# Two-layer decoder trunk on one core: FFN gate and up products with the weights stationary in nine of eleven steps

## The chip, the cores and the metric

One core of one Trainium2 chip runs the whole kernel. The metric is device time in microseconds (us) of one execution. Engines are called as the profile calls them: PE is TensorE's matrix products, PEld its weight loads, DVE is VectorE, ACT is ScalarE, POOL is GpSimd and SP is SyncE, which issues the weight DMAs.

## The reference, cut to what matters

The input is 256 tokens of 1024 channels; there are two layers. A layer is: a SwiGLU FFN, a mixer with two kinds of attention, a second SwiGLU FFN, and a gated embedding. The change touches only the two FFNs of each layer:

```python
def swiglu(x, w_gu, w_down):
    g, u = jnp.split(x @ w_gu, 2, axis=-1)
    return (jax.nn.silu(g) * u) @ w_down

f = swiglu(rms_norm(h, ffn1_pre_g[i]), ffn1_w_gu[i], ffn1_w_down[i])
h = h + 0.5 * rms_norm(f, ffn1_post_g[i])
```

`w_gu` is 1024 x 5632 and `w_down` 2816 x 1024, all in float32. The row scale of `rms_norm`, one number r per token, is not applied to x: the kernel multiplies the results g and u by it. The channel gain is folded into the weights.

## The kernel before, in words

**Numbers.** A float32 matrix is split in two parts that the PE takes at its fast float32 form: `w_hi` is the rounded weight, `w_lo` the rest, and the same for x (`x_hi`, `x_lo`) and the gated product (`ht_hi`, `ht_lo`). `exact` (line 1336) makes three matmuls of each block: hi by hi (line 1338), hi by lo (line 1339), lo by hi (line 1340), accumulated in PSUM. Of a matmul's operands one is stationary, a 128 x 128 block that a weight load (PEld) puts into the array, and one is moving and streams through it column by column. Here x is stationary and the weights move, 512 columns a matmul, so every matmul has a load of its own.

**Tiling.** Tokens are 2 tiles of 128 (t). Weights come from HBM in units of 1 MB, in 3 slots of `raw`; SP loads unit u when the splitting of unit u - 3 is done. For each unit ACT makes `w_hi` (`high`, line 591) and DVE then `w_lo` (`low`, line 1002); ACT waits for `units_used`, that is for PE to be done with the unit that was in the slot. PE waits for `split_done` (`begin`, line 1367).

**The FFN's steps.** The 2816 hidden channels are 11 steps (NC) of 256. A step c is `step` (line 1457): `gate_up` on its first unit (k blocks 0 to 3 of 8), the transposes of step c - 1 (`turn_ht`), `gate_up` on its second unit (k blocks 4 to 7), and `down` of step c - 1. `gate_up` does 24 matmuls a unit: for t, for k, three. PSUM bank 4 gets tile 0 (256 columns of gate, 256 of up) and bank 5 gets tile 1. `down` is 24 more. Steps 2 to 9 are a hardware loop; the first and the last step are written out.

**The gated product.** When tile t is done, ACT computes silu(r g) from PSUM with r as its per-partition scale (`silu`, line 684), and DVE multiplies it by r u (`product`, line 1041): tokens are the partitions. `down` wants the hidden channels as partitions, so PE transposes the 128 x 256 product of both tiles with four 128 x 128 transposes (`turn_ht`, line 1409), ACT copies them rounded into `ht_hi` (`high_ht`, line 673) and DVE the rest into `ht_lo` (`low_ht`, line 1030).

**Order.** The order is written out by hand. In the loop ACT does: high of the down unit, `high_ht`, high of the next first unit, two `silu`, high of the next second unit. DVE does the same with `low`, `low_ht`, `product`.

Of the kernel before, what the change touches and what calls it, by code (L numbers as in the profile page):

```python
# [73 lines left out]
def trunk_kernel(nc, a, out):  # L74
    with ExitStack() as ctx:
# [3 lines left out]
        def sem(name):  # L79
            return ctx.enter_context(nc.semaphore(name))  # L80
# [496 lines left out]
        def _(act):  # L577
# [92 lines left out]
                high_inputs(i, q, 1, (1,))  # L670
                square_pre(i, n + 1, 1)

            def high_ht(i, f, c):
                act.wait_ge(ht_turned, 2 * HTS * i + HTS * f + c + 1)
                act.activation(ht_hi[:, :, :], bank(HT_BANK).rearrange("p (k n) -> p k n", k=2),  # L675
                               ACT.Copy).then_inc(ht_high, 1)

            def high_last_ht(i, f, t):
                toks = slice(t * P, (t + 1) * P)
                act.wait_ge(ht_turned, 2 * HTS * i + HTS * f + NC + t)  # L680
                act.activation(x_hi[:, 0:2, toks], bank(HT_BANK).rearrange("p (k n) -> p k n", k=2)[:, :, toks],
                               ACT.Copy).then_inc(ht_high, 1)

            def silu(i, f, step, u, t, c=0):
                wait_product(act, gu_done, 2 * NC * i + NC * f + step + 1, i, u, t, c)
                act.activation(glu[:, t, 0, :], bank(GU_BANK[t])[:, 0:FC], ACT.Silu,  # L686
                               scale=r_pre[:, t:t + 1]).then_inc(silu_done, 1)

            def ffn(i, f, u0, g0, next_unit, loads, embedding):

                act.wait_ge(pre_scale, 8 * i + 4 * f + 1)
                silu(i, f, 0, u0 + 1, 0)
# [5 lines left out]
                with act.Fori(1, NC - 1) as c:  # L698
# [3 lines left out]
                    for t in range(TT):  # L702
                        silu(i, f, c, u0, t, c)
# [5 lines left out]
                for t in range(TT):  # L709
                    silu(i, f, NC - 1, u0 + 3 * NC - 3, t)  # L710
                high_last_ht(i, f, 0)
                next_unit()
                high_last_ht(i, f, 1)
# [238 lines left out]
        def _(dve):  # L952
# [94 lines left out]
            def ffn(i, f, u0, g0, next_unit):  # L1047
                product(i, f, 0, 0)
                low(i, u0 + 3, g0 + 4, halves=(0,))
                product(i, f, 0, 1)  # L1050
                low(i, u0 + 3, g0 + 4, halves=(1,))
                with dve.Fori(1, NC - 1) as c:
                    low(i, u0 + 1, c=c)
                    low_ht(i, f, c - 1)
                    low(i, u0 + 2, g0, c=c)
                    for t in range(TT):
                        product(i, f, c, t)
# [4 lines left out]
                low_ht(i, f, NC - 2)  # L1062
# [270 lines left out]

        @block.tensor
        def _(pe):
            def exact(dst, x_h, x_l, w_h, w_l, first, last):

                pe.matmul(dst, x_h, w_h, start=first, stop=False)  # L1338
                pe.matmul(dst, x_h, w_l, start=False, stop=False)  # L1339
                return pe.matmul(dst, x_l, w_h, start=False, stop=last)  # L1340

            def wide(s, dst, xh, xl, k0, t, first, last, before=None):

# [62 lines left out]
                        elif s == 1 and done is not None:  # L1406
                            mm.then_inc(done, 1)

            def turn_ht(i, f, c):
                pe.wait_ge(prod_done, 4 * NC * i + 2 * NC * f + 2 * c + 2)  # L1410
                for k in range(2):
                    for t in range(TT):
                        mm = pe.transpose(bank(HT_BANK)[:, k * SEQ + t * P:k * SEQ + (t + 1) * P],  # L1413
                                          glu[:, t, 1, k * P:(k + 1) * P], ident[:, :])
                mm.then_inc(ht_turned, 1)
# [19 lines left out]
                return wait  # L1435

            def ffn(i, f, q, u0, before_last):
                def gate_up(u, half, step, c=0):

                    begin(i, u, c)  # L1440
                    for t in range(TT):
                        if half == 0:

                            pe.wait_ge(prod_done, 4 * NC * i + 2 * NC * f + 2 * step + t - 1)
                        mm = wide(slot(u), bank(GU_BANK[t]), x_hi, x_lo, 4 * half, t, half == 0, half == 1)
                        if half == 1 and t == 0:
                            mm.then_inc(gu_done, 1)
                    mm.then_inc(units_used, 1)
# [47 lines left out]
                turn_ht(i, f, NC - 2)  # L1496
# [277 lines left out]
```

## Time and profile before

| | us |
|---|---|
| median of 3 runs | 1201.45 (1201.3 to 1202.21) |
| the profiled execution, its own time | 1202.05 |
| its span, first to last instruction | 1200.3 |
| PE busy | 1185.5 |
| PEld busy | 968.0 |
| DVE busy | 753.5 |
| ACT busy | 684.5 |

The profiled execution took 1.75 us more than its span; this lies around the first and the last instruction. A matmul's duration in the profile runs from when it starts to when its last result is out, so durations of matmuls that follow each other overlap: the pace is read from starts, or from a stretch divided by the matmuls in it. PEld runs beside PE. In a timeline a row with xN merges N instructions of one line.

### The profile page before, as it was taken

The numbers are of one execution on the slowest core, as the hardware profiler recorded it, in microseconds if no ns is written. First come the engines' busy times: TensorE is split into PE (matmuls) and PEld (weight loads), VectorE is DVE, ScalarE is ACT, GpSimd is POOL, SyncE is SP. The second block draws the span as 40 slices with busy tenths as digits, with TensorE's granted clock in tenths as the row PEclk, the third lists the DMA queues.
The fourth block names the chain that finished last, engine by engine and source line by source line (L and its number), as shares of the span: only waits on it lengthen the run. The fifth ranks groups of instructions, "written<-read, shape, count | busy, mean of one in ns | idle before, by whom it ended". The sixth has DMA issues, their size and how long they took to land.

```text
span 1200.3 us, 15956 instructions
## 1 busy us (share of the span) xinstructions
PE 1185.5 (99%) x5585; PEld 968.0 (81%) x5585; DVE 753.5 (63%) x1086; ACT 684.5 (57%) x1122; POOL 91.5 (8%) x153
## 2 busy tenths in 40 slices
PE   8999999999999999999999999999999999999997
PEld 6888888877778888888878888878877888888886
DVE  5655656677667755565775555575966676555566
ACT  6644556666665654454674554475656756455455
POOL 3000000042000000000100000010600000000001
PEclk9999999999999999999999999999999999999999
DMA  7756555553345565655546555746344456555550
GB/s 259 231 186 203 178 194 198 194 175 118 129 176 175 179 193 188 200 180 206 176 146 207 181 194 182 240 163 202 121 138 141 175 175 211 176 179 193 185 193 35
DMA packets 138607, 215.33 MB, mean 179 GB/s; under 512 B 6914, under 2 KB 97860, under 8 KB 138564
## 3 DMA queue, kind: packets, MB, share of 16 engines
q1 hardware_dynamic: 135840, 208.70, 52.2%
q10 hardware_dynamic: 2660, 6.06, 1.5%
q8 instruction: 27, 0.44, 0.1%
q14 instruction: 16, 0.13, 0.0%
q0 software_dynamic: 64, 0.00, 0.0%
HBM read 213.68 MB, written 1.05 MB: 179 GB/s over the span
## 4 chain that ended last, share of the span: by engine, by line
PE 92%; DVE 3%; ACT 3%; issue 1%; DMA 1%; POOL 0%; SPq 0%; DVEq 0%; POOLq 0%; ACTq 0%
PE ps L1338 29%; PE ps L1340 28%; PE ps L1339 28%; DVE w_lo L1016 2%; PE ps L1413 1%; PE ps L1385 1%; ACT w_hi L607 1%; PE ps L1507 1%; ACT prob L740 1%; PE ps L1553 1%; DMA raw<-in_w_ple_proj 1%; PE ps L1540 0%; PE ps L1526 0%; ACT w_hi L604 0%; DVE neg_max L1195 0%
## 5 line engine op out<-in xcount | busy, mean ns | idle before, releaser
L1338 PE MATMUL ps<-w_hi,x_hi 128*128 128x512 f32 x1216 | 486.7, 400 | 1.4 <-DVE x_lo L1027 0.7
L1340 PE MATMUL ps<-w_hi,x_lo 128*128 128x512 f32 x1216 | 475.5, 391 | 0.0
L1339 PE MATMUL ps<-w_lo,x_hi 128*128 128x512 f32 x1216 | 474.2, 390 | 0.0
L1016 DVE SCALAR_TENSOR_TENSOR w_lo<-raw,g_layer,w_hi 128x512 fp32r<-128x512 f32 (+1 forms) x524 | 392.9, 808 | 82.9 <-ACT w_hi L607 82.1
L607 ACT ACTIVATE w_hi<-raw,g_layer 128x512 fp32r<-128x512 f32 (+1 forms) x524 | 346.5, 732 | 15.6 <-PE ps L1340 15.5
L1338 PEld LDWEIGHTS ps<-w_hi,x_hi 128*128 128x128 f32 x1216 | 228.5, 188 | 55.4 <-issue 5.3
L1340 PEld LDWEIGHTS ps<-w_hi,x_lo 128*128 128x128 f32 x1216 | 228.2, 188 | 49.2
L1339 PEld LDWEIGHTS ps<-w_lo,x_hi 128*128 128x128 f32 x1216 | 228.8, 188 | 43.7
L1013 DVE TENSOR_TENSOR w_lo<-raw,w_hi 128x1024 fp32r<-128x1024 f32 x114 | 134.6, 1221 | 81.6 <-ACT w_hi L604 81.6
L604 ACT ACTIVATE w_hi<-raw 128x1024 fp32r<-128x1024 f32 x114 | 114.7, 1052 | 103.5 <-PE ps L1340 103.5
L1338 PE MATMUL ps<-w_hi,ht_hi 128*128 128x512 f32 x320 | 125.0, 390 | 0.0
L1340 PE MATMUL ps<-w_hi,ht_lo 128*128 128x512 f32 x320 | 124.6, 389 | 0.0
L1339 PE MATMUL ps<-w_lo,ht_hi 128*128 128x512 f32 x320 | 124.5, 389 | 0.0
L675 ACT ACTIVATE ht_hi<-ps 128x512 fp32r<-128x512 f32 x40 | 23.9, 598 | 145.2 <-PE ps L1413 145.2
L1032 DVE TENSOR_TENSOR ht_lo<-ps,ht_hi 128x512 fp32r<-128x512 f32 x40 | 27.6, 691 | 112.3 <-ACT ht_hi L675 112.3
L686 ACT ACTIVATE glu<-ps,r_pre 128x256 f32<-128x256 f32 x88 | 41.1, 467 | 85.8 <-PE ps L1340 85.8
L1043 DVE SCALAR_TENSOR_TENSOR glu<-ps,r_pre,glu 128x256 f32<-128x256 f32 x88 | 42.3, 480 | 46.2 <-ACT glu L686 46.2
L1340 PEld LDWEIGHTS ps<-w_hi,ht_lo 128*128 128x128 f32 x320 | 60.1, 188 | 12.5
L1339 PEld LDWEIGHTS ps<-w_lo,ht_hi 128*128 128x128 f32 x320 | 60.1, 188 | 12.4
L1338 PEld LDWEIGHTS ps<-w_hi,ht_hi 128*128 128x128 f32 x320 | 60.1, 188 | 12.3
L639 ACT ACTIVATE x_hi<-ps 128x512 fp32r<-128x512 f32 x40 | 23.7, 595 | 37.6 <-PE ps L1385 37.6
L495 POOL TENSOR_TENSOR ms_post<-mean_post,eps_half 128x1 f32<-128x1 f32 x8 | 2.2, 271 | 555.8 <-ACT tmp L656 555.8
(193 smaller groups left out, 749.4 us busy)
## 6 DMA issues: line engine op xcount, KB each, us to landing
raw<-in_ffn_w_gu SPq DMA_DIRECT2D x170, 512.0 KB, 4.6
raw<-in_ffn_w_down SPq DMA_DIRECT2D x88, 512.0 KB, 4.0
raw<-in_w_in SPq DMA_DIRECT2D x80, 512.0 KB, 4.5
raw<-in_w_out SPq DMA_DIRECT2D x16, 512.0 KB, 3.7
raw<-in_w_ple_gate SPq DMA_DIRECT2D x16, 512.0 KB, 4.1
raw<-in_w_branch_sb SPq DMA_DIRECT2D x8, 512.0 KB, 3.7
raw<-in_w_branch_diff SPq DMA_DIRECT2D x8, 512.0 KB, 3.8
raw<-in_ffn_w_gu SPq DMA_DIRECT2D x12, 256.0 KB, 7.2
```

Of the source, the lines that this page charges most:

```text
L604: last = act.activation(w_hi[:, s, part], raw[:, s, part], ACT.Copy)
L607: last = act.activation(w_hi[:, s, part], raw[:, s, part], ACT.Copy, scale=g_layer[:, g:g + 1])
L639: act.activation(x_hi[:, 4 * n:4 * n + 4, t * P:(t + 1) * P], x_bank(i, q, idx).rearrange("p (k n) -> p k n", k=4), ACT.Copy).then_inc(x_h ...
L675: act.activation(ht_hi[:, :, :], bank(HT_BANK).rearrange("p (k n) -> p k n", k=2), ACT.Copy).then_inc(ht_high, 1)
L686: act.activation(glu[:, t, 0, :], bank(GU_BANK[t])[:, 0:FC], ACT.Silu, scale=r_pre[:, t:t + 1]).then_inc(silu_done, 1)
L1013: last = dve.tensor_tensor(w_lo[:, s, part], raw[:, s, part], whi[:, part], ALU.subtract)
L1016: last = dve.scalar_tensor_tensor(out=w_lo[:, s, part], in0=raw[:, s, part], scalar=g_layer[:, g:g + 1], in1=whi[:, part], op0=ALU.mult, o ...
L1032: dve.tensor_tensor(ht_lo[:, :, :], bank(HT_BANK).rearrange("p (k n) -> p k n", k=2), ht_hi[:, :, :].bitcast(F32), ALU.subtract).then_inc( ...
L1043: dve.scalar_tensor_tensor(out=glu[:, t, 1, :], in0=bank(GU_BANK[t])[:, FC:2 * FC], scalar=r_pre[:, t:t + 1], in1=glu[:, t, 0, :], op0=ALU ...
L1338: pe.matmul(dst, x_h, w_h, start=first, stop=False)
L1339: pe.matmul(dst, x_h, w_l, start=False, stop=False)
L1340: return pe.matmul(dst, x_l, w_h, start=False, stop=last)
```

## The change

In steps 1 to 9 of each FFN (36 of the 44 steps of the whole kernel) gate and up are computed the other way round: the weights are the stationary operand, 128 hidden channels at a time, and x moves, all 256 tokens. `flat_gate_up` goes over four groups j of 128 hidden channels in a unit (two of gate, into bank 4, two of up, into bank 5) and the four k blocks, with three 256-column matmuls each: 48 matmuls a unit and not 24. The result has the hidden channels as partitions, so nothing is transposed: `turn_ht` is gone from steps 2 to 10, and `high_ht` and `low_ht` read `glu` in SBUF and not PSUM. Step 0 and step 10 stay as they were; step 0's product is still transposed, in `turn_first_ht`.

r now varies along the columns. Once an FFN, DVE spreads r over 128 columns (`spread_r`), PE transposes it for both tiles into bank 7, ahead of step 0's four transposes, and ACT copies it to `r_cols`, which lies in `prob`. `flat_gate` on DVE is g times r, then, after ACT's silu in place, times r, then times u: three 512-element operations where two of 256 were.

```diff
+HT_TURNS = 3
+FLAT = NC - 2
...
+        R_BANK = 7
+        flat_g, flat_u = (bank(b).rearrange("p (k n) -> p k n", k=2) for b in GU_BANK)
...
+            def high_ht(i, f, c):
+                act.wait_ge(prod_done, 4 * NC * i + 2 * NC * f + 2 * c + 2)
+                act.activation(ht_hi[:, :, :], glu_u, ACT.Copy).then_inc(ht_high, 1)
...
+            def keep_r(i, f):
+                act.wait_ge(r_turned, 2 * i + f + 1)
+                act.activation(r_cols[:, 0, :], bank(R_BANK)[:, 0:SEQ], ACT.Copy).then_inc(r_kept, 1)
+
+            def flat_silu(i, f, c):
+                act.wait_ge(prod_done, 4 * NC * i + 2 * NC * f + 2 * c + 1)
+                act.activation(glu_g, glu_g, ACT.Silu).then_inc(silu_done, 2)
...
+            def spread_r(i, f):
+                if (i, f) == (0, 0):
+                    dve.wait_ge(const_all, 1)
+                dve.tensor_copy(r_spread, r_pre[:, :].rearrange("p (t o) -> p t o", o=1).to_broadcast([P, TT, P])
+                                ).then_inc(r_wide, 1)
+
+            def flat_gate(i, f, c, u0):
+                n = FLAT * (2 * i + f)
+                wide_r = r_cols.to_broadcast([P, 2, SEQ])
+                dve.wait_ge(gu_done, 2 * NC * i + NC * f + c + 1)
+                dve.tensor_tensor(glu_g, flat_g, wide_r, ALU.mult).then_inc(prod_done, 1)
+                dve.wait_ge(silu_done, 4 * NC * i + 2 * NC * f + 2 * c + 2)
+                dve.tensor_tensor(glu_g, glu_g, wide_r, ALU.mult).then_inc(silu_scaled, 1)
+                dve.wait_ge(units_used, UNITS * i + 3 * c + u0 + 1 + SLOTS)
+                dve.wait_ge(silu_scaled, n + c)
+                dve.tensor_tensor(glu_u, flat_u, glu_g, ALU.mult).then_inc(prod_done, 1)
...
-            def turn_ht(i, f, c):
-                pe.wait_ge(prod_done, 4 * NC * i + 2 * NC * f + 2 * c + 2)
+            def turn_first_ht(i, f):
+                pe.wait_ge(r_wide, 2 * i + f + 1)
+                for t in range(TT):
+                    mm = pe.transpose(bank(R_BANK)[:, t * P:(t + 1) * P], r_spread[:, t, :], ident[:, :])
+                mm.then_inc(r_turned, 1)
                 for k in range(2):
                     for t in range(TT):
                         mm = pe.transpose(bank(HT_BANK)[:, k * SEQ + t * P:k * SEQ + (t + 1) * P],
...
+                def flat_gate_up(u, half, step, c=0):
+
+                    begin(i, u, c)
+                    s = slot(u)
+                    for j in range(4):
+                        if half == 0 and j % 2 == 0:
+
+                            pe.wait_ge(prod_done, 4 * NC * i + 2 * NC * f + 2 * step + j // 2 - 1)
+                        dst = bank(GU_BANK[j // 2])[:, j % 2 * SEQ:(j % 2 + 1) * SEQ]
+                        for k in range(4):
+                            cols, kx = slice(k * W + j * P, k * W + (j + 1) * P), 4 * half + k
+                            mm = exact(dst, w_hi[:, s, cols], w_lo[:, s, cols], x_hi[:, kx, :], x_lo[:, kx, :],
+                                       half == 0 and j % 2 == 0 and k == 0, half == 1 and j % 2 == 1 and k == 3,
+                                       skip_group_check=True)
+                        if half == 1 and j == 1:
+                            mm.then_inc(gu_done, 1)
+                    mm.then_inc(units_used, 1)
+
...
-                    gate_up(u0 - 1, 0, c, at)
+                    flat_gate_up(u0 - 1, 0, c, at)
...
-                    turn_ht(i, f, c - 1)
-                    gate_up(u0, 1, c, at)
+                    if first:
+                        turn_first_ht(i, f)
+                    flat_gate_up(u0, 1, c, at)
                     down(u0 + 1, c - 1, first=first, c=at)
```

PE in the loop, where the first unit of a step ends and the second begins, before (a row's `ps<-w_hi,x_hi` has the moving operand first, then the stationary one; `split_done` is the wait for the unit's weights):

```order
L1339 MATMUL ps<-w_lo,x_hi 128x512
L1340 MATMUL ps<-w_hi,x_lo 128x512
L1410 ISA
L1413 MATMUL ps<-ident,glu 128x128 [waits prod_done]
L1413 MATMUL ps<-ident,glu 128x128 x3
L1369 REGISTER_ALU
L1338 MATMUL ps<-w_hi,x_hi 128x512 [waits split_done]
L1339 MATMUL ps<-w_lo,x_hi 128x512
```

and with the change:

```order
L1391 MATMUL ps<-x_lo,w_hi 128x256
L1392 MATMUL ps<-x_hi,w_lo 128x256
L1421 REGISTER_ALU
L1390 MATMUL ps<-x_hi,w_hi 128x256 [waits split_done]
L1391 MATMUL ps<-x_lo,w_hi 128x256
L1392 MATMUL ps<-x_hi,w_lo 128x256
```

The four transposes and their wait are gone, the moving operand is x, and each unit has 48 such rows where it had 24.

DVE in the loop, where a step's product is made, before:

```order
L1016 SCALAR_TENSOR_TENSOR w_lo<-raw,g_layer,w_hi 128x512
L1042 ISA
L1043 SCALAR_TENSOR_TENSOR glu<-ps,r_pre,glu 128x256 [waits silu_done]
L1042 REGISTER_ALU
L1043 SCALAR_TENSOR_TENSOR glu<-ps,r_pre,glu 128x256 [waits silu_done]
L1007 REGISTER_ALU
L1016 SCALAR_TENSOR_TENSOR w_lo<-raw,g_layer,w_hi 128x512 [waits hi_ready]
```

and with the change:

```order
L1045 SCALAR_TENSOR_TENSOR w_lo<-raw,g_layer,w_hi 128x512
L1073 REGISTER_ALU
L1074 TENSOR_TENSOR glu<-ps,prob 128x512 [waits gu_done]
L1075 ISA
L1076 TENSOR_TENSOR glu<-glu,prob 128x512 [waits silu_done]
L1077 ISA
L1079 TENSOR_TENSOR glu<-ps,glu 128x512 [waits silu_scaled,units_used]
L1036 REGISTER_ALU
L1045 SCALAR_TENSOR_TENSOR w_lo<-raw,g_layer,w_hi 128x512 [waits hi_ready]
```

Three operations stand between the two splittings of weights where two stood, and the last of them waits for the end of the second unit.

## Rows read from the trace of the kernel before

**Rows 1.** The page: busy time by engine, granted clock in 40 slices, chain by engine.
```profile
PE 1185.5 (99%) x5585; PEld 968.0 (81%) x5585; DVE 753.5 (63%) x1086; ACT 684.5 (57%) x1122; POOL 91.5 (8%) x153
...
PEclk9999999999999999999999999999999999999999
...
PE 92%; DVE 3%; ACT 3%; issue 1%; DMA 1%; POOL 0%; SPq 0%; DVEq 0%; POOLq 0%; ACTq 0%
```

**Rows 2.** Windows: one step of the first FFN, from transposes to transposes (columns in its heading).
```profile
core 0: us, PE busy (x) PEld busy (x) DVE busy (x) ACT busy (x) POOL busy (x), PEclk, DMA share, GB/s
51.30:68.10 16.80, 16.80 (x78) 13.90 (x77) 9.41 (x13) 8.34 (x13) 0.00 (x0) 1.00 0.58 190
```

**Rows 3.** Timeline of PE, around the four transposes: start us, us, engine, line.
```profile
67.55 0.39 PE L1340 MATMUL ps<-w_hi,x_lo 128*128 128x512 f32 x1
67.78 0.60 PE L1413 MATMUL ps<-ident,glu 128*128 128x128 f32 x4
68.13 0.48 PE L1338 MATMUL ps<-w_hi,x_hi 128*128 128x512 f32 x1
68.45 0.40 PE L1339 MATMUL ps<-w_lo,x_hi 128*128 128x512 f32 x1
```

**Rows 4.** Groups by line and shape in that step (xcount | busy us, mean ns | idle).
```profile
L1339 PE MATMUL ps<-w_lo,x_hi 128*128 128x512 f32 x16 | 6.2, 389 | 0.0
...
L1043 DVE SCALAR_TENSOR_TENSOR glu<-ps,r_pre,glu 128x256 f32<-128x256 f32 x2 | 1.0, 481 | 1.0 <-ACT glu L686 1.0
L686 ACT ACTIVATE glu<-ps,r_pre 128x256 f32<-128x256 f32 x2 | 0.9, 464 | 2.1 <-PE ps L1340 2.1
L1032 DVE TENSOR_TENSOR ht_lo<-ps,ht_hi 128x512 fp32r<-128x512 f32 x1 | 0.7, 691 | 3.1 <-ACT ht_hi L675 3.1
...
L675 ACT ACTIVATE ht_hi<-ps 128x512 fp32r<-128x512 f32 x1 | 0.6, 598 | 3.9 <-PE ps L1413 3.9
```

**Rows 5.** Lines 1540 and 1541, duration ns min/median/max.
```profile
L1540 PE MATMUL ps<-sp_hi,neg_tri x16: 333/360/388, 254.7 to 905.2; 128*128 128x384 f32 x16
...
L1541 PE MATMUL ps<-sp_hi,neg_one x16: 220/220/220, 254.8 to 905.4; 128*128 128x128 f32 x16
...
L1541 PE MATMUL ps<-sp_lo,neg_one x16: 223/224/228, 255.1 to 905.7; 128*128 128x128 f32 x16
```

**Rows 6.** Timeline of PE where these two lines alternate.
```profile
254.66 0.33 PE L1540 MATMUL ps<-sp_hi,neg_tri 128*128 128x384 f32 x1
254.84 0.22 PE L1541 MATMUL ps<-sp_hi,neg_one 128*128 128x128 f32 x1
254.89 0.39 PE L1540 MATMUL ps<-sp_lo,neg_tri 128*128 128x384 f32 x1
```

**Rows 7.** Timeline of the weight loads around lines 1585 and 1587.
```profile
301.94 0.30 PEld L1585 LDWEIGHTS ps<-v_df,mixed_t 128*128 128x128 f32 x2
302.16 0.30 PEld L1587 LDWEIGHTS ps<-v_df,mixed_t 128*128 128x128 f32 x2
```

**Rows 8.** Timeline of PE and its loads, a product with a late next load.
```profile
244.71 0.39 PE L1339 MATMUL ps<-w_lo,x_hi 128*128 128x512 f32 x1
244.71 0.19 PEld L1340 LDWEIGHTS ps<-w_hi,x_lo 128*128 128x128 f32 x1
244.94 0.39 PE L1340 MATMUL ps<-w_hi,x_lo 128*128 128x512 f32 x1
245.16 0.12 PEld L1513 LDWEIGHTS ps<-mask_sb,ident_b 128*128 128x128 bf16 x2 [0.26 <-issue]
```

**Rows 9.** Waits of PE: us in total, times, longest us.
```profile
PE ps L1338 <- DVE glu L1043: 0.4, 1, 0.4
```

**Rows 10.** Timelines of DVE, then PE, around the end of a gate-and-up product.
```profile
70.27 2.74 DVE L1016 SCALAR_TENSOR_TENSOR w_lo<-raw,g_layer,w_hi 128x512 fp32r<-128x512 f32 x4 [0.53 <-ACT w_hi L607]
72.93 0.48 DVE L1043 SCALAR_TENSOR_TENSOR glu<-ps,r_pre,glu 128x256 f32<-128x256 f32 x1
...
73.70 0.39 PE L1338 MATMUL ps<-w_hi,ht_hi 128*128 128x512 f32 x1
```

More of the change, by code:

```diff
@@ L168, in trunk_kernel @@
         rope_s = sb("rope_s", [P, TT, 64])
+        glu_g, glu_u = glu[:, 0, :, :], glu[:, 1, :, :]
+        r_spread = mixed_t[:, 0:SEQ].rearrange("p (t n) -> p t n", t=TT)
+        r_cols = prob[:, 0:1, 0:SEQ]
         e_ple = gates[:, 1, :, :]
@@ L190, in trunk_kernel @@
         prod_done = sem("prod_done")
+        silu_scaled = sem("silu_scaled")
+        r_wide = sem("r_wide")
+        r_turned = sem("r_turned")
+        r_kept = sem("r_kept")
         ht_turned = sem("ht_turned")
@@ L671, in boundary, with high_first_ht @@
                 square_pre(i, n + 1, 1)
-            def high_ht(i, f, c):
-                act.wait_ge(ht_turned, 2 * HTS * i + HTS * f + c + 1)
+            def high_first_ht(i, f):
+                act.wait_ge(ht_turned, HT_TURNS * (2 * i + f) + 1)
                 act.activation(ht_hi[:, :, :], bank(HT_BANK).rearrange("p (k n) -> p k n", k=2),
                                ACT.Copy).then_inc(ht_high, 1)
+            def high_ht(i, f, c):
[7 more added lines that the diff above has]
+                act.activation(glu_g, glu_g, ACT.Silu).then_inc(silu_done, 2)
             def high_last_ht(i, f, t):
                 toks = slice(t * P, (t + 1) * P)
-                act.wait_ge(ht_turned, 2 * HTS * i + HTS * f + NC + t)
+                act.wait_ge(ht_turned, HT_TURNS * (2 * i + f) + 2 + t)
                 act.activation(x_hi[:, 0:2, toks], bank(HT_BANK).rearrange("p (k n) -> p k n", k=2)[:, :, toks],
@@ L697, in ffn @@
                 embedding()
-                with act.Fori(1, NC - 1) as c:
+                high(i, u0 + 4)
+                keep_r(i, f)
+                high_first_ht(i, f)
+                high(i, u0 + 5, g0)
+                flat_silu(i, f, 1)
+                high(i, u0 + 6, g0 + 4)
+                with act.Fori(2, NC - 1) as c:
                     high(i, u0 + 1, c=c)
@@ L701, in ffn @@
                     high(i, u0 + 2, g0, c=c)
-                    for t in range(TT):
-                        silu(i, f, c, u0, t, c)
+                    flat_silu(i, f, c)
                     high(i, u0 + 3, g0 + 4, c=c)
@@ L708, in ffn @@
                 high(i, u0 + 3 * NC - 1)
-                for t in range(TT):
-                    silu(i, f, NC - 1, u0 + 3 * NC - 3, t)
+                silu(i, f, NC - 1, u0 + 3 * NC - 3, 0)
+                act.wait_ge(ht_split, 2 * HTS * i + HTS * f + NC - 1)
+                silu(i, f, NC - 1, u0 + 3 * NC - 3, 1)
                 high_last_ht(i, f, 0)
@@ L1028, in low_inputs, with low_ht @@
                                       x_hi[part].bitcast(F32), ALU.subtract).then_inc(x_split, 1)
-            def low_ht(i, f, c):
+            def low_ht(i, f, c, src):
                 dve.wait_ge(ht_high, 2 * HTS * i + HTS * f + c + 1)
-                dve.tensor_tensor(ht_lo[:, :, :], bank(HT_BANK).rearrange("p (k n) -> p k n", k=2),
-                                  ht_hi[:, :, :].bitcast(F32), ALU.subtract).then_inc(ht_split, 1)
+                dve.tensor_tensor(ht_lo[:, :, :], src, ht_hi[:, :, :].bitcast(F32), ALU.subtract
+                                  ).then_inc(ht_split, 1)
+            def spread_r(i, f):
[13 more added lines that the diff above has]
+                dve.tensor_tensor(glu_u, flat_u, glu_g, ALU.mult).then_inc(prod_done, 1)
             def low_last_ht(i, f, t):
@@ L1050, in ffn @@
                 product(i, f, 0, 1)
+                spread_r(i, f)
                 low(i, u0 + 3, g0 + 4, halves=(1,))
-                with dve.Fori(1, NC - 1) as c:
+                low(i, u0 + 4)
+                low_ht(i, f, 0, bank(HT_BANK).rearrange("p (k n) -> p k n", k=2))
+                low(i, u0 + 5, g0)
+                dve.wait_ge(r_kept, 2 * i + f + 1)
+                flat_gate(i, f, 1, u0)
+                low(i, u0 + 6, g0 + 4)
+                with dve.Fori(2, NC - 1) as c:
                     low(i, u0 + 1, c=c)
-                    low_ht(i, f, c - 1)
+                    low_ht(i, f, c - 1, glu_u)
                     low(i, u0 + 2, g0, c=c)
-                    for t in range(TT):
-                        product(i, f, c, t)
+                    flat_gate(i, f, c, u0)
                     low(i, u0 + 3, g0 + 4, c=c)
@@ L1061, in ffn @@
                 low(i, u0 + 3 * NC - 2)
-                low_ht(i, f, NC - 2)
+                low_ht(i, f, NC - 2, glu_u)
                 low(i, u0 + 3 * NC - 1)
@@ L1335, in _, with exact @@
         def _(pe):
[L1336 to L1340, printed above, removed]
+            def exact(dst, x_h, x_l, w_h, w_l, first, last, **group):
+                pe.matmul(dst, x_h, w_h, start=first, stop=False, **group)
+                pe.matmul(dst, x_h, w_l, start=False, stop=False, **group)
+                return pe.matmul(dst, x_l, w_h, start=False, stop=last, **group)
             def wide(s, dst, xh, xl, k0, t, first, last, before=None):
@@ L1495, in ffn @@
                 gate_up(u0 + 3 * NC - 4, 0, NC - 1)
-                turn_ht(i, f, NC - 2)
                 gate_up(u0 + 3 * NC - 3, 1, NC - 1)
```

## The prediction

> **What bounds the kernel now.** I read the page first: PE is busy for 99% of the span, its clock is at full rate in all 40 slices, and the chain that ended last lies for 92% on PE [rows 1]. Then one step of an FFN, as a window: PE is busy all of its 16.80 us at granted clock 1.00, which is the 2.4 GHz level, while DVE has 9.41 and ACT 8.34 us of work [rows 2]. The waits say the same from the other side: of all DVE products of gate and up in the whole kernel, one was waited for by PE, for 0.4 us [rows 9]. So the FFNs, 44 steps of 16.8 us, are bound by what PE has to stream, and the change is worth what it does to PE's stream, unless it makes another engine late.
>
> **The prices on PE.** A step is 72 matmuls of 512 columns and four transposes. From line 1340 before the transposes to the second matmul behind them it is 68.45 - 67.55 = 0.90 us [rows 3]. Two 512-column matmuls of that at 0.227 leave 0.446 for four transposes, 111 ns each; (16.80 - 0.446) / 72 = 227.2 ns is then the pace of a 512-column matmul, which agrees with the 0.227 taken. Its 512 columns at 2.4 GHz are 213.3 ns, so 13.9 ns come on top.
>
> **Removed.** 36 steps lose their four transposes, and these wait in PE's own stream, with nothing beside them: 36 x 0.446 = 16.1 us.
>
> **Added.** Two transposes of r in each of 4 FFNs: 8 x 0.111 = 0.9 us.
>
> **Changed.** In 36 steps two units of 24 matmuls become 48 of half the columns: 36 x 48 = 1728 matmuls of 512 columns at 227.2 ns become 3456 of 256 at s. The sum hangs on s, and the trace has no 256-column matmul of this kind. With D = 1728 x (2s - 227.2) ns and 15.2 us net of the transposes gained, even is at 2s = 227.2 + 8.8, s = 118.0 ns.
>
> The nearest rows are lines 1540 and 1541, of the same number format, with a load of a full 128 x 128 block for each: 384 columns and 128. A matmul's duration is its pace and a fixed run-out: 389 ns for 512 columns at a pace of 227 leaves 162 [rows 4]. The 384-column matmul has 333 ns where nothing holds it up (the minimum; the longer ones stood waiting for their load), so a pace of 171, and the 128-column ones 220 and 224, so 58 and 62 [rows 5]. The starts agree: 254.66 to 254.84 is 0.18 for 384 columns and 254.84 to 254.89 0.05 for 128 [rows 6]. What comes on top of the columns' own time is 5 to 9 ns at 128, 11 at 384, 14 at 512: it grows with the length, and is not a fixed fee. Halfway between 60 and 171 lies 115.5 ns, and I take this. D = 1728 x (231.0 - 227.2) = 6.6 us.
>
> The **bounds** of s. From below the loads: every matmul has its own, and where loads bound the pace (lines 1585 and 1587, 128 columns) two of them take 0.22 us, so 111 ns each [rows 7]. s can't be under this: D = 1728 x (222 - 227.2) = -9.0 us. From above, the whole 13.9 ns as a fee for each matmul: 106.7 + 13.9 = 120.6, D = 24.2 us. It is no fee for a load beside the stream: where the next load came late, at 245.16 for a matmul that started at 244.94, the matmul had the usual 0.39 us [rows 8].
>
> Two rules of the Trainium skill bear on this. The page "TensorE: Matmul & The Clock Gate", section "Back-to-back issue gap", gives N / 2.4 + 2.5 ns for a matmul of N columns in isolation, which is 109.2 ns at 256 and would by itself make D -15.2 us, 1172 us in all; for 512 columns it says 215.8, and the trace disagrees, at 227.2. The same page, in its part 3 under "The mechanism", says that a load overlaps with matmuls in flight only where their row groups differ; by it 1728 more loads of 111 ns would cost 192 us, but the trace disagrees: a load starts at 244.71, with the matmul of 244.71 running, and 213 and 111 ns don't fit one after the other into a pace of 227 [rows 8].
>
> **DVE and ACT.** In a flat step DVE has three operations of 512 elements at 0.69 us, the price of the nearest row, `ht_lo`, in place of two of 0.48, so 1.1 us more; ACT has one silu of 512 at about 0.60, as `ht_hi`, in place of two of 0.47 [rows 4]. DVE comes to 10.5 us in a step of nearly 17: it hides, and costs nothing. The order counts, however. The gate half is done 24 matmuls, 2.8 us, before the second unit ends. DVE must first finish the splitting that stood at 70.27 to 73.01, while the second unit ended near 73.70 [rows 10]; in the change that splitting starts some half a microsecond earlier, since ACT no longer waits for the transposes ahead of it. So g times r starts about 1 us before the end of the unit, and with 0.69 + 0.60 + 0.69 + 0.69 us and the handovers the product is there some 2 us behind it. PE starts the next step after `down`, 24 x 0.227 = 5.4 us behind the same end, and asks there only for g times r to be done, since that frees the gate bank; the product it asks for 24 matmuls later, at 8.2 us. So 6 us are to spare. If this cover were gone, each microsecond of lateness would cost 36 us. Behind the product in DVE's queue stands the splitting of the next second unit, which PE wants some 11 us after the end of this one: covered as well. SP issues a load when a splitting is done, in an order that doesn't change; the shares of all queues stay as they are.
>
> The new waits of PE, for r to be spread (once an FFN), stand behind a unit of 5.5 us that starts when the last product is nearly done; I cost them at 0, at most 0.3 us each. `ht_hi` and `ht_lo` no longer depend on PE and come earlier; nothing was waiting for them.
>
> **Sum.** 6.6 - 16.1 + 0.9 = -8.6 us. The profiled execution, 1202.05 us, becomes 1193.4; it stood 0.6 above the median, so about 1193 against 1201.45.
>
> **The rivals.**
> - *A fixed fee for each matmul* (the slower one). Place: the 48 matmuls of a flat unit on PE; price: 13.9 ns for each of 1728 more, s = 120.6. Against it are the 128-column rows, which leave no room for 13.9, for it that they are few and stand between stalls, and that 384 columns already show 11. It decides from s = 118.0 up. It gives 1202.05 - 15.2 + 24.2 = 1211.0.
> - *The loads set the pace*, and the 256 columns flow with hardly anything on top: s = 111, 1202.05 - 15.2 - 9.0 = 1177.8. For it speaks the load pace, just under the stream's; against it that all streams of this format show something on top, 11 ns at 384. (The first rule of the Trainium skill above belongs here: its 109.2 ns lies just under this floor.)
> - *DVE is late*: the product ends more than 8.2 us behind the second unit. Each microsecond over it costs 36 us, so one microsecond gives 1193.4 + 36 = 1229. Nothing in the rows makes it so late: DVE would need 6 us more than counted.
> - *Loads don't overlap*: 1728 x 0.111 = 192 us more, 1385 us; excluded by the pace of 227, chance 0.
>
> **How the numbers follow.** The forecast, s from 113 to 117.3, has 0.48; loads at the pace and s under 113 have 0.12; s from 117.3 to 118.7, no change, 0.10; the fixed fee, with what lies above 118.7, 0.27; a late engine 0.03. What a measurement of this kernel can tell from no change is 0.2%, 2.4 us, which is 0.7 ns of s on either side of 118.0. Faster is then 0.60, the same 0.10, slower 0.30. As both signs have a chance, the likeliest case's own range is 1185 (s = 113) to 1199 (s = 117.3). The range of 8 in 10 leaves out the tip of the loads' case and what lies beyond the fixed fee: 1179 to 1212.
>
> **What would show it.** In the profile after: in the middle of a flat step the starts of 256-column matmuls, 115 or 116 ns apart (111: loads; 120 to 121: the fee). The period of a step, 48 of 512 columns gone: 96 x 0.1155 + 24 x 0.2272 = 16.54 us and not 16.80. Durations of 277 ns. No wait of PE on a DVE product, DVE busy about 10.5 us in a step. Wrong would be: a period over 16.8 with starts at the pace (the fee is real), or idle time before the first matmul of a step (DVE or ACT is late).

## The result, and the profile after

The kernel got slower: 1208.81 us median of 5 runs (1207.7 to 1209.22) against 1202.21 for the kernel before in the same comparison, a ratio of 1.0057, 95% interval 1.0046 to 1.0067. The profiled execution of the changed kernel took 1207.83 us, with a span of 1206.1; that of the kernel before 1202.05 and 1200.3.

The page of the changed kernel, with the lines that answer to [rows 1] and the first of the three groups of new matmuls with its load (columns as in the rows ahead of the prediction):

```profile
span 1206.1 us, 19135 instructions
...
PE 1191.2 (99%) x7177; PEld 1044.3 (87%) x7177; DVE 790.6 (66%) x1126; ACT 683.8 (57%) x1090; POOL 92.7 (8%) x153
...
PEclk9999999999999999999999999999999999999999
...
PE 92%; DVE 3%; ACT 3%; DMA 1%; issue 1%; POOL 0%; DVEq 0%; POOLq 0%; ACTq 0%
...
L1390 PE MATMUL ps<-x_hi,w_hi 128*128 128x256 f32 x1152 | 326.2, 283 | 0.4 <-DVE glu L1089 0.4
...
L1390 PEld LDWEIGHTS ps<-x_hi,w_hi 128*128 128x128 f32 x1152 | 221.0, 192 | 2.2 <-DVE w_lo L1045 0.8
```

PE bounds it as before, at full clock. PE has 1592 instructions more; each of them brought a load, and PEld went from 968.0 to 1044.3 us.

One flat step, a window from the first matmul of a step to the first of the next, answers to [rows 2]:

```profile
core 0: us, PE busy (x) PEld busy (x) DVE busy (x) ACT busy (x) POOL busy (x), PEclk, DMA share, GB/s
45.28:62.26 16.98, 16.98 (x121) 16.02 (x120) 10.43 (x14) 8.29 (x12) 0.00 (x0) 1.00 0.58 186
```

It takes 16.98 us, where a step took 16.80, and PE is busy in all of it. 24 of its matmuls are those of `down`, 5.44 us at the 226.7 ns that a 512-column matmul takes in a row (run e4 below); the rest is 96 matmuls of 256 columns in 11.54 us, 120.2 ns each. The timeline of PE at the start of such a step shows the same pace, from the last matmul of `down` on:

```profile
96.00 0.39 PE L1392 MATMUL ps<-w_hi,ht_lo 128*128 128x512 f32 x1
96.22 0.28 PE L1390 MATMUL ps<-x_hi,w_hi 128*128 128x256 f32 x1
96.34 0.28 PE L1391 MATMUL ps<-x_lo,w_hi 128*128 128x256 f32 x1
96.45 0.28 PE L1392 MATMUL ps<-x_hi,w_lo 128*128 128x256 f32 x1
96.58 0.28 PE L1390 MATMUL ps<-x_hi,w_hi 128*128 128x256 f32 x1
...
96.94 0.28 PE L1390 MATMUL ps<-x_hi,w_hi 128*128 128x256 f32 x1
```

From 96.22 to 96.94 six of them start in 0.72 us, 120 ns apart. Durations of line 1390, ns min/median/max:

```profile
L1390 PEld LDWEIGHTS ps<-x_hi,w_hi x1152: 186/192/193, 27.5 to 1146.4; 128*128 128x128 f32 x192
L1390 PE MATMUL ps<-x_hi,w_hi x1152: 277/283/365, 27.7 to 1146.5; 128*128 128x256 f32 x192
...
L1390 PE MATMUL ps<-w_hi,x_hi x640: 387/389/506, 15.2 to 1198.0; 128*128 128x512 f32 x160
```

The median is 283, and with the 162 ns of run-out that the 512-column row gives (389 - 227) that is a pace of 121. In the loop nothing but the pace is new. PE's waits answer to [rows 9]:

```profile
PE ps L1390 <- DVE w_lo L1023: 0.9, 1, 0.9
...
PE ps L1390 <- DVE glu L1089: 0.4, 1, 0.4
PE ps L1390 <- DVE w_lo L1045: 0.2, 1, 0.2
```

The one wait on a product of gate and up is the one that was there before, 0.4 us, and comes in step 1 of one FFN, behind step 0's product.

The account closes. 36 steps at 16.98 for 16.805 (the starts of nine successive steps of the first FFN lie 134.45 us apart before and 135.84 now) are +6.3 us, the eight transposes of r +0.9. Against that the first flat step begins 1.05 us earlier in this execution, since the very first loads landed at other times; it varies from execution to execution (in e10, which has the same matmuls as the changed kernel, that step begins 1.3 us later than here), and isn't put down to the change. Before, then after, the first matmul of step 1:

```profile
28.70 0.40 PE L1338 MATMUL ps<-w_hi,x_hi 128*128 128x512 f32 x1
```

```profile
27.65 0.28 PE L1390 MATMUL ps<-x_hi,w_hi 128*128 128x256 f32 x1
```

6.3 + 0.9 - 1.05 = 6.2 us; the spans differ by 5.8, and 0.4 us stay unaccounted for.

### The profile page after: what moved, and what is told of

The parts are those of the page before. It is cut to its first block, busy times and chain, and to the rows that moved or that the text cites. A ratio compares the mean times of both kernels' runs of the same rounds, so it can differ in the third digit from the quotient of the medians.

```text
span 1206.1 us, 19135 instructions
## 1 busy us (share of the span) xinstructions
PE 1191.2 (99%) x7177; PEld 1044.3 (87%) x7177; DVE 790.6 (66%) x1126; ACT 683.8 (57%) x1090; POOL 92.7 (8%) x153
## 3 DMA queue, kind: packets, MB, share of 16 engines
HBM read 213.68 MB, written 1.05 MB: 178 GB/s over the span
## 4 chain that ended last, share of the span: by engine, by line
PE 92%; DVE 3%; ACT 3%; DMA 1%; issue 1%; POOL 0%; DVEq 0%; POOLq 0%; ACTq 0%
PE ps L1390 29%; PE ps L1392 29%; PE ps L1391 28%; DVE w_lo L1045 2%; PE ps L1437 1%; ACT w_hi L618 1%; PE ps L1580 1%; ACT prob L769 1%; PE ps L1626 1%; DMA h<-in_x 0%; PE ps L1613 0%; PE ps L1599 0%; ACT w_hi L615 0%; DVE neg_max L1247 0%; PE ps L1586 0%
## 5 line engine op out<-in xcount | busy, mean ns | idle before, releaser
L1390 PE MATMUL ps<-x_hi,w_hi 128*128 128x256 f32 x1152 | 326.2, 283 | 0.4 <-DVE glu L1089 0.4
L1392 PE MATMUL ps<-x_hi,w_lo 128*128 128x256 f32 x1152 | 326.0, 283 | 0.0
L1391 PE MATMUL ps<-x_lo,w_hi 128*128 128x256 f32 x1152 | 326.0, 283 | 0.0
L1390 PE MATMUL ps<-w_hi,x_hi 128*128 128x512 f32 x640 | 258.5, 404 | 1.0 <-DVE x_lo L1056 0.7
L1392 PE MATMUL ps<-w_hi,x_lo 128*128 128x512 f32 x640 | 250.3, 391 | 0.0
L1391 PE MATMUL ps<-w_lo,x_hi 128*128 128x512 f32 x640 | 249.8, 390 | 0.0
L1390 PEld LDWEIGHTS ps<-x_hi,w_hi 128*128 128x128 f32 x1152 | 221.0, 192 | 2.2 <-DVE w_lo L1045 0.8
L1391 PEld LDWEIGHTS ps<-x_lo,w_hi 128*128 128x128 f32 x1152 | 221.0, 192 | 1.3
L1392 PEld LDWEIGHTS ps<-x_hi,w_lo 128*128 128x128 f32 x1152 | 221.0, 192 | 0.0
L1390 PEld LDWEIGHTS ps<-w_hi,x_hi 128*128 128x128 f32 x640 | 120.2, 188 | 33.4 <-issue 5.2
L1391 PEld LDWEIGHTS ps<-w_lo,x_hi 128*128 128x128 f32 x640 | 120.5, 188 | 21.9
```

The source lines that it names most:

```text
L1390: pe.matmul(dst, x_h, w_h, start=first, stop=False, **group)
L1391: pe.matmul(dst, x_h, w_l, start=False, stop=False, **group)
L1392: return pe.matmul(dst, x_l, w_h, start=False, stop=last, **group)
```

## The experiments

Each kernel is built on one of the two. Where a pace is given for the flat steps, it is the step less 5.44 us for `down`, divided by the 96 matmuls. In the changed kernel and its variants `down` really takes 5.47 to 5.50 us, from its first matmul to the first of the next step, since its first matmuls, behind shorter ones, are a little slow; so these paces are up to 0.6 ns too high (120.0 by the starts above, for 120.2). e1, e2, e3, e5, e6 and e9, which leave out or falsify part of the work, ran once each; there it is the step in the trace that carries the argument, and it is the same in steps 2 to 9 of every FFN to 0.04 us. Theory A said that the weight loads set the pace of 120, theory B that each matmul has a fixed fee of 13.3 ns on top of its columns.

### e1: 192 moving columns

```diff
-dst = bank(GU_BANK[j // 2])[:, j % 2 * SEQ:(j % 2 + 1) * SEQ]
+dst = bank(GU_BANK[j // 2])[:, j % 2 * SEQ:j % 2 * SEQ + 192]
...
-mm = exact(dst, w_hi[:, s, cols], w_lo[:, s, cols], x_hi[:, kx, :], x_lo[:, kx, :],
+mm = exact(dst, w_hi[:, s, cols], w_lo[:, s, cols], x_hi[:, kx, 0:192], x_lo[:, kx, 0:192],
```

> The changed kernel with 192 of the 256 columns moving in every matmul of the flat steps (64 tokens of gate and up are left out). Theory A, the loads set the pace: a load starts behind the start of the matmul before it and the next matmul can't start until 117 ns later, so the pace stays at 120 ns and the time at 1208. Theory B, a fixed fee of 13.3 ns on top of the columns: 80.0 + 13.3 = 93, held at the 111 ns at which loads were seen to follow each other, so 1208 - 3456 x 0.009 = 1177.

Measured: 1179.6 us. One flat step, in the columns of the window above:

```profile
45.30:61.47 16.17, 16.17 (x122) 15.22 (x121) 10.33 (x14) 8.22 (x12) 0.00 (x0) 1.00 0.62 196
```

(16.17 - 5.44) / 96 = 111.8 ns. Theory A falls: at 120 ns the loads don't hold the pace, since with a shorter stream it drops. It drops to the floor of 111 that [rows 7] gave for loads, and not to the 93 of the columns and the fee. The load floor of the prediction was right, and at 256 columns it doesn't decide.

### e2: stationary blocks of 96 columns

```diff
-dst = bank(GU_BANK[j // 2])[:, j % 2 * SEQ:(j % 2 + 1) * SEQ]
+dst = bank(GU_BANK[j // 2])[0:96, j % 2 * SEQ:(j % 2 + 1) * SEQ]
...
-cols, kx = slice(k * W + j * P, k * W + (j + 1) * P), 4 * half + k
+cols, kx = slice(k * W + j * P, k * W + j * P + 96), 4 * half + k
```

> The changed kernel with stationary blocks of 96 columns, not 128, in the flat steps (32 of each 128 hidden channels are left out); the moving side keeps its 256 columns. Theory A, loads set the pace: a shorter load is out of the way, and the stream's own pace shows, 113.3 ns, as in the first matmul of each flat step: 1208 - 3456 x 0.0067 = 1185. Theory B, a fixed fee for each matmul: 120 ns and 1208 stay.

Measured: 1194.8 us.

```profile
45.30:61.93 16.63, 16.63 (x123) 15.62 (x122) 10.40 (x14) 8.29 (x13) 0.00 (x0) 1.00 0.63 196
```

(16.63 - 5.44) / 96 = 116.6 ns, between the two: neither theory as it stands. The stationary block, whose load is shorter now, has a part in the fee. I made theory C of it: 0.104 ns for each stationary column.

### e3: 320 moving columns

```diff
-dst = bank(GU_BANK[j // 2])[:, j % 2 * SEQ:(j % 2 + 1) * SEQ]
+dst = bank(GU_BANK[j // 2])[:, j % 2 * 192:j % 2 * 192 + 320]
...
+xh, xl = (x[:, kx:kx + 2, :].rearrange("p k n -> p (k n)")[:, 0:320] for x in (x_hi, x_lo))
...
-mm = exact(dst, w_hi[:, s, cols], w_lo[:, s, cols], x_hi[:, kx, :], x_lo[:, kx, :],
+mm = exact(dst, w_hi[:, s, cols], w_lo[:, s, cols], xh, xl,
```

> The changed kernel with 320 moving columns in every matmul of the flat steps (64 of them doubled work into columns that overlap, so gate and up are not what they should be). What the stream itself costs beyond the loads: Theory A, in proportion to the columns, as 226.7 ns for 512 and 113.3 for 256 make it: 141.7 ns, 1208 + 3456 x 0.0217 = 1283. Theory B, the columns and a fixed 13.3 ns: 146.7 ns, 1208 + 3456 x 0.0267 = 1300.

Measured: 1301.5 us.

```profile
45.30:64.84 19.54, 19.54 (x122) 18.58 (x121) 10.42 (x14) 8.35 (x13) 0.00 (x0) 1.00 0.50 167
```

(19.54 - 5.44) / 96 = 146.9 ns, theory B's figure to 0.2 ns, and 1301.5 for its 1300. With a full block, what comes on top of the columns' time at 2.4 GHz is 13.5 ns at 256 columns (120.2 - 106.7), 13.6 at 320 (146.9 - 133.3) and 13.4 at 512 (226.7 - 213.3): a fee that doesn't grow with the length. The columns' time itself shows in these runs: (226.7 - 120.2) / 256 is 0.416 ns a column, one at each tick of 2.4 GHz. What the engine does in the fee stays open.

### e4: the kernel before without its transposes

```diff
 def high_ht(i, f, c):
-    act.wait_ge(ht_turned, 2 * HTS * i + HTS * f + c + 1)
-    act.activation(ht_hi[:, :, :], bank(HT_BANK).rearrange("p (k n) -> p k n", k=2),
-                   ACT.Copy).then_inc(ht_high, 1)
+    act.wait_ge(prod_done, 4 * NC * i + 2 * NC * f + 2 * c + 2)
+    act.activation(ht_hi[:, :, :], glu[:, :, 1, :], ACT.Copy).then_inc(ht_high, 1)
...
-                    turn_ht(i, f, c - 1)
...
-                turn_ht(i, f, NC - 2)
```

> The kernel before, without the four transposes in steps 1 to 10: ht_hi and ht_lo are made from the product in SBUF as it lies, so down multiplies with untransposed data. It tests the term for the removed work alone. Both theories: 40 groups x 0.446 = 17.8 us less than before, 1184. If the transposes had been partly hidden, less than that would go.

Measured: 1181.98 us against 1201.2 beside it, ratio 0.9841 (0.9824 to 0.9857).

```profile
62.00:78.32 16.32, 16.32 (x74) 13.52 (x73) 9.31 (x14) 8.49 (x14) 0.00 (x0) 1.00 0.58 194
```

The step is 16.32 us, 72 matmuls at 226.7 ns. A group of four transposes was worth 16.80 - 16.32 = 0.48 us and not 0.446: 19.2 us for 40 groups where 17.8 were expected. They stood wholly in PE's stream, and the matmuls behind them took a little over 227 ns as well (line 1339 with 0.40 in [rows 3], where 0.39 is usual).

### e5 and e6: stationary blocks of 64 columns, with 256 and with 192 moving

```diff
-dst = bank(GU_BANK[j // 2])[:, j % 2 * SEQ:(j % 2 + 1) * SEQ]
+dst = bank(GU_BANK[j // 2])[0:64, j % 2 * SEQ:(j % 2 + 1) * SEQ]
...
-cols, kx = slice(k * W + j * P, k * W + (j + 1) * P), 4 * half + k
+cols, kx = slice(k * W + j * P, k * W + j * P + 64), 4 * half + k
```

e6 has the 192 columns of e1 as well.

> The changed kernel with stationary blocks of 64 columns in the flat steps (half of the hidden channels are left out), 256 moving columns. Theory B, the fee belongs to the matmul: it doesn't fall further than at 96 columns, where the mean pace of a step was 116.4 ns. Theory C, the fee is in proportion to the stationary block, 0.104 ns for each of its columns (13.3 at 128, 10 at 96): 106.7 + 6.7 = 113.3 ns, 1208 - 3456 x 0.0067 = 1185.

> The same with 192 moving columns as well. At 192 columns and a full block the pace was 111.7 ns, where the columns and the fee would have been 93: the loads held it. If that floor belongs to the number of columns loaded, half the block frees it: theory C gives 80 + 6.7 = 86.7 ns and 1208 - 3456 x 0.0333 = 1093, theory B with the fee of the 96-column run 80 + 9.7 = 89.7 and 1103. If the floor is a time for any load, 111.7 ns and 1180 stay.

Measured: 1185.5 us for e5, as theory C has it, which is no longer theory B's 1208; and 1102.0 for e6, near the 1103 that a fee of 9.7 ns, that of the 96-column run, gave. A step of e5, then one of e6:

```profile
45.30:61.65 16.35, 16.35 (x123) 15.34 (x121) 10.33 (x14) 8.29 (x13) 0.00 (x0) 1.00 0.62 196
```

```profile
45.30:59.29 13.99, 13.99 (x123) 12.98 (x122) 10.33 (x15) 8.18 (x13) 0.00 (x0) 1.00 0.68 228
```

The paces are (16.35 - 5.44) / 96 = 113.6 ns and (13.99 - 5.44) / 96 = 89.1. Durations of line 1390 and of its load in e5:

```profile
L1390 PEld LDWEIGHTS ps<-x_hi,w_hi x1152: 133/134/137, 27.6 to 1124.1; 128*64 128x64 f32 x192
L1390 PE MATMUL ps<-x_hi,w_hi x1152: 276/276/363, 27.8 to 1124.2; 128*64 128x256 f32 x192
```

With half a block the load is 58 ns shorter (134 for 192 in the changed kernel) and the fee at 256 columns is half, 6.9 ns; at 192 columns it is 9.1, so C isn't exact. The load floor of e1 is gone: it goes with the number of columns loaded, not with a load as such.

### e7 and e8: one load of w_hi for both parts of x

A third way to do the whole computation, in steps 2 to 9: w_hi moves x_hi and x_lo together, 512 columns into a whole bank, and w_lo moves x_hi alone. ACT copies the lo half of each bank to SBUF and DVE adds it to the hi half. x_hi and x_lo lie side by side for that.

```diff
-        x_hi = sb("x_hi", [P, KD, SEQ], F32R)
-        x_lo = sb("x_lo", [P, KD, SEQ], F32R)
+        x_both = sb("x_both", [P, KD, 2, SEQ], F32R)
+        x_hi, x_lo = x_both[:, :, 0, :], x_both[:, :, 1, :]
...
+                    for j in range(4):
+                        dst = bank(WIDE_BANK[j])
+                        for k in range(4):
+                            cols, kx = slice(k * W + j * P, k * W + (j + 1) * P), 4 * half + k
+                            pe.matmul(dst, w_hi[:, s, cols], x_both[:, kx, :, :].rearrange("p a n -> p (a n)"),
+                                      start=half == 0 and k == 0, stop=False, skip_group_check=True)
+                            mm = pe.matmul(dst[:, 0:SEQ], w_lo[:, s, cols], x_hi[:, kx, :],
+                                           start=False, stop=half == 1 and k == 3, skip_group_check=True)
```

> The whole computation, a third way: in steps 2 to 9 of each FFN w_hi is loaded once for x_hi and x_lo together, 512 moving columns into a whole bank, and w_lo moves x_hi, 256 columns; ACT and DVE add the two halves of each bank. 32 matmuls a unit, not 48. Theory B, a fee of 13.3 ns for each matmul with a full block: 226.7 + 120.0 = 346.7 ns for each of 32 pairs in a step, a step of 11.09 + 5.45 = 16.55 us against 16.98, 1208 - 32 x 0.43 = 1194, under the kernel before by 7. Theory A, the 256-column matmul runs at 113.3 when its neighbours leave its load more time: 340 ns, a step of 16.33, 1187. A wait of PE on the product, since DVE has five operations where it had three and ACT three where it had one: above 1200.

Measured: 1202.74 us against 1202.22 beside it, ratio 1.0004 (0.9994 to 1.0013): not to be told from the kernel before.

```profile
62.00:78.79 16.79, 16.79 (x90) 14.30 (x89) 11.62 (x17) 9.26 (x14) 0.00 (x0) 1.00 0.56 187
```

A pair takes (16.79 - 5.44) / 32 = 354.7 ns, 8 more than theory B had. PE has no idle time, and DVE 11.62 us of work; so it is PE's own pace. The timeline of PE, two pairs:

```profile
66.03 0.40 PE L1551 MATMUL ps<-x_both,w_hi 128*128 128x512 f32 x1
66.26 0.28 PE L1553 MATMUL ps<-x_both,w_lo 128*128 128x256 f32 x1
66.38 0.40 PE L1551 MATMUL ps<-x_both,w_hi 128*128 128x512 f32 x1
66.62 0.28 PE L1553 MATMUL ps<-x_both,w_lo 128*128 128x256 f32 x1
```

A 512-column matmul is followed after 0.23 to 0.24 us, not 0.227, and has 0.40 for 0.39. e8 has the same matmuls in another order:

```diff
-                    for j in range(4):
-                        dst = bank(WIDE_BANK[j])
-                        for k in range(4):
+                    for js in ((0, 1), (2, 3)):
+                        for part in range(2):
+                            for j in js:
+                                dst = bank(WIDE_BANK[j])
+                                for k in range(4):
...
+                                    if part == 0:
```

> The third way once more, with the same matmuls in another order: in a unit, for the two gate groups and then for the two up groups, first the eight of 512 columns and then the eight of 256, where 512 and 256 took turns. The taking turns cost 354.4 ns a pair, 8 more than 226.7 + 120.0. Theory D, it is the change of length from one matmul to the next that costs these 8 ns: 346.7 a pair but for the few changes that are left, a step of 16.6 us against 16.79, 1202.5 - 32 x 0.2 = 1196, under both kernels. If it is the w_hi load for two parts of x, or ACT's and DVE's reading of more PSUM banks, 16.79 and 1202.5 stay.

Measured: 1196.72 us against 1201.64 beside it, ratio 0.9959 (0.9946 to 0.9973). This version computes everything and beats both kernels, the one before by 4.9 us.

```profile
62.00:78.61 16.61, 16.61 (x90) 14.34 (x89) 11.63 (x17) 9.27 (x14) 0.00 (x0) 1.00 0.59 189
```

```profile
65.65 1.53 PE L1554 MATMUL ps<-x_both,w_hi 128*128 128x512 f32 x6
67.02 1.11 PE L1558 MATMUL ps<-x_both,w_lo 128*128 128x256 f32 x8
67.97 2.00 PE L1554 MATMUL ps<-x_both,w_hi 128*128 128x512 f32 x8
69.82 0.40 PE L1558 MATMUL ps<-x_both,w_lo 128*128 128x256 f32 x2
```

A pair is (16.61 - 5.44) / 32 = 349.1 ns, so of the 8 ns in excess, 5.6 went with the order alone. What the order changed is how often a matmul follows one of another length, and the starts show the cost there: the eight of 256 columns take 0.95 us (67.02 to 67.97), 119 ns each, and the eight of 512 behind them 1.85 us (67.97 to 69.82), 231 each, for 120 and 226.7 in a long row. The short matmul behind a long one loses nothing; the long ones behind a short one do. That w_hi and w_lo take turns as the loaded block doesn't cost this: they do so in the changed kernel too, at 120 ns. A part of the excess, 2 ns a pair in e7 and 1 in e8, even stands in `down`, which takes 5.50 and 5.47 us there. That reading more PSUM banks cost PE these 5.6 ns falls, since e8 reads them too.

### e9: the kernel before with 64 stationary columns

```diff
-cols, toks = slice(k * W, (k + 1) * W), slice(t * P, (t + 1) * P)
+cols, toks = slice(k * W, (k + 1) * W), slice(t * P, t * P + rows)
...
-mm = wide(slot(u), bank(GU_BANK[t]), x_hi, x_lo, 4 * half, t, half == 0, half == 1)
+mm = wide(slot(u), bank(GU_BANK[t])[0:64], x_hi, x_lo, 4 * half, t, half == 0, half == 1, rows=64)
```

> The kernel before, with only the first 64 of each 128 tokens stationary in the gate and up matmuls of the FFN steps 1 to 10 (the other tokens' gate and up are left out). It asks whether the fee follows the stationary block at 512 columns too. Theory C, 0.104 ns for each stationary column: 213.3 + 6.7 = 220.0 ns for 48 of the 72 matmuls of a step, 16.81 - 48 x 0.0067 = 16.48 us, and 40 steps of that, 1202 - 13 = 1189. Theory B, the fee belongs to the length of the stream or to the matmul: 16.81 and 1202 stay.

Measured: 1206.9 us, 5.3 more than the kernel before with less work.

```profile
62.00:78.92 16.92, 16.92 (x77) 11.39 (x76) 9.41 (x14) 8.33 (x13) 0.00 (x0) 1.00 0.56 185
```

```profile
70.28 0.40 PE L1338 MATMUL ps<-w_hi,x_hi 128*64 128x512 f32 x1
70.51 0.39 PE L1339 MATMUL ps<-w_lo,x_hi 128*64 128x512 f32 x1
70.74 0.39 PE L1340 MATMUL ps<-w_hi,x_lo 128*64 128x512 f32 x1
70.96 0.39 PE L1338 MATMUL ps<-w_hi,x_hi 128*64 128x512 f32 x1
71.19 0.40 PE L1339 MATMUL ps<-w_lo,x_hi 128*64 128x512 f32 x1
71.42 0.39 PE L1340 MATMUL ps<-w_hi,x_lo 128*64 128x512 f32 x1
71.66 0.40 PE L1338 MATMUL ps<-w_hi,x_hi 128*64 128x512 f32 x1
```

16.92 us for a step, where theory C had 16.48 and theory B 16.81; both fall here. Six matmuls take 1.38 us (70.28 to 71.66), 230 ns each for 226.7, in the middle of a unit, where all 24 loads have 64 columns and all streams 512; `down`, with full blocks, keeps its 5.44 us. So it isn't a change of length that costs here: theory C holds for the 256-column streams of e2 and e5, and at 512 columns the shorter load makes the pace worse, not better. 40 such steps are 4.6 of the 5.3 us.

### e10: more work on DVE

```diff
                 dve.wait_ge(silu_scaled, n + c)
+                spare = w_att[:, :, :].rearrange("p t (a n) -> p (t a) n", a=3)[:, 0:4, :]
+                eye = ident[:, :].rearrange("p (o n) -> p o n", o=1).to_broadcast([P, 4, P])
+                for e in range(6):
+                    dve.tensor_tensor(spare, eye, eye, ALU.mult).then_inc(extra, 1)
+                    dve.wait_ge(extra, 6 * (n + c) - 5 + e)
                 dve.tensor_tensor(glu_u, flat_u, glu_g, ALU.mult).then_inc(prod_done, 1)
```

> The changed kernel with six more 512-element multiplications on DVE in each flat step, into a spare tile, just ahead of the product's last operation. It asks whether DVE's added work is hidden. If it is, as the count of 6 us to spare says: six times 0.69 make the product and all splitting behind it 4.1 us later, PE waits for none of it, the step stays 16.98 us and the time 1208.5. If DVE is nearer to the bound than counted: each microsecond over the cover costs 36 us, up to 36 x 4.1 = 148 us more.

Measured: 1208.34 us, ratio to the kernel before 1.0057 (1.004 to 1.0074), as the changed kernel has.

```profile
45.30:62.28 16.98, 16.98 (x122) 16.02 (x121) 14.87 (x21) 8.30 (x12) 0.00 (x0) 1.00 0.57 187
```

The step is 16.98 us with DVE busy for 14.87 of them. DVE's work is hidden, with more than 4 us to spare.

## Why the prediction was wrong, point by point

**What bounds the kernel** was right: PE before and after, at full clock, and no other engine is waited for.

**Removed** was right in mechanism and sized 7% too low: 0.48 us a group in e4 where 0.446 was taken, 17.3 us for 36 groups and not 16.1.

**Added** was right. The two transposes of r and the four of step 0's product in the changed kernel:

```profile
33.41 0.38 PE L1464 MATMUL ps<-ident,mixed_t 128*128 128x128 f32 x2
33.62 0.60 PE L1468 MATMUL ps<-ident,glu 128*128 128x128 f32 x4
```

0.21 us for the two, and nobody waits for r.

**Changed** is the step that failed: "Halfway between 60 and 171 lies 115.5 ns, and I take this". The pace is 120.2 ns. With it and the pace of 226.7, D = 1728 x (240.4 - 226.7) = 23.7 us where 6.6 were summed. 23.7 - 17.3 + 0.9 = 7.3 us is what the account of the two traces found in the steps and the transposes of r (7.2); between the medians are 6.6. The sum missed D by 17.1 us, and the transposes by 1.2 only. What misled was the sentence behind it, that what comes on top "grows with the length, and is not a fixed fee". The 128-column row from which it came was a short matmul between longer ones. The changed kernel has such a place too, the first 256-column matmul of a step, behind `down`. Alone in its window it has

```profile
L1390 PE MATMUL ps<-x_hi,w_hi x1: 277/277/277, 96.2 to 96.2; 128*128 128x256 f32 x1
```

which by the run-out is a pace of 277 - 162 = 115, just the figure interpolated, while the median of all is 283, which is 121. So a short matmul behind a longer one doesn't show the pace of a row of short ones. (That the 128-column row misled in just this way is argued from the likeness; no run has 128 columns of this kind in a row without the loads' floor.) Had the 384-column row been taken for what it was, 171 with 160 of columns, a fee of 11 and with it 118 would have come out, which is no gain.

**The bounds** held. The upper one, the whole 13.9 ns as a fee, was almost the truth: 120.6 for 120.2. The lower one, 111 for the loads, is a real floor (111.8 in e1), but that the excess is no loss to a load beside the stream, as the prediction read [rows 8], doesn't hold as it stands: half a block makes the excess smaller (e5), so the block that is loaded does enter. [rows 8] gives the duration of one matmul, and that doesn't tell when the next could have started.

**The rules.** A row of 256-column matmuls goes at 120.2 ns. By the Trainium skill, page "TensorE: Matmul & The Clock Gate", section "Back-to-back issue gap", the formula for a matmul in isolation makes it 109.2; the trace disagrees, as it did at 512 columns. The section says of a stream of loads and matmuls that both set the spacing, and there e1 and e5 agree. In those 120.2 ns lies a load of 111 beside 107 of columns, so the two overlap. The same page of the Trainium skill, part 3, "The mechanism", has a sentence by which they would do so only with different row groups, and with it the trace disagrees here too; but the section also lets a load go ahead that targets the background weight buffer, which the prediction left out, and with that the trace is in keeping.

**DVE and ACT** were right: DVE 10.43 us in a step for 10.5, and the product in time. DVE around the end of a second unit, then the first matmul of `down`:

```profile
55.26 0.68 DVE L1074 TENSOR_TENSOR glu<-ps,prob 128x512 f32<-128x512 f32 x1
56.71 0.69 DVE L1076 TENSOR_TENSOR glu<-glu,prob 128x512 f32<-128x512 f32 x1 [0.76 <-ACT glu L699]
57.50 0.69 DVE L1079 TENSOR_TENSOR glu<-ps,glu 128x512 f32<-128x512 f32 x1
...
56.80 0.40 PE L1390 MATMUL ps<-w_hi,ht_hi 128*128 128x512 f32 x1
```

The product is done at 58.19, 1.4 us behind the end of the unit at 56.80; 2 were counted. e10 confirms the cover.

**The rivals.** The fixed fee is what happened: it had 1211.0 us for the profiled execution, which took 1207.83. Of the 3.2 us between, 1.2 are the transposes, worth 17.3 and not 16.1, 0.5 the D of 23.7 for 24.2, and 1.05 the earlier first flat step, which is luck. It had 0.27 and should have had the most: 512 columns had 14 ns on top and 384 had 11, and only the 128-column rows had less. The measured time lay inside the range and on the wrong side.

## What to carry to other kernels

Cutting matmuls in half to save another kind of PE work is only a gain if what comes on top of each of them is smaller than the saving: here 48 more matmuls a step at 13.5 ns, 0.65 us, against 0.48 us of transposes. Read the pace of a matmul from many of the same length in a row, never from a single one among others. And once matmuls of two lengths are needed, run those of one length together: that alone was worth 0.18 us a step, 5.8 us in all, from e7 to e8, and made a version that beats both kernels out of one that beat only the changed one.

## What the runs showed of the hardware that was not expected

- At 256, 320 and 512 moving columns of this format with a full stationary block, in a row, the pace is the columns at 2.4 GHz and 13.4 to 13.6 ns: 120.2, 146.9 and 226.7.
- With 96 and 64 stationary columns the pace at 256 is 116.6 and 113.6. At 512 columns with 64 stationary ones it got worse, 16.92 us a step for 16.80 (e9). There the loads and the streams of a whole unit have one length each, so it isn't a change of length; why a shorter load helps at 256 columns and hurts at 512 stays open.
- A matmul with a full block has a floor of 111.8 ns (e1), which is gone with half a block (89.1, e6).
- Where matmuls of 512 and 256 columns take turns, a pair takes 354.7 ns, in groups of eight 349.1, where 346.9 would be the sum of the two paces. The cost falls on the long matmuls behind a short one (e8: 231 ns in a group). What in the engine makes it wasn't tried.
